# Rows of per-token numbers made by TensorE transposes of a broadcast column instead of products with the identity

## The reference, cut to what matters

```python
def _modulated_norm(h, gain, shift, scale):
    return _rms_norm(h, gain) * (1.0 + scale) + shift      # 1/root of the mean square, per token

def _l2_normalize(x):                                       # 1/length, per token and head
    xf = x.astype(jnp.float32)
    return (xf * lax.rsqrt(jnp.sum(xf * xf, axis=-1, keepdims=True) + EPS)).astype(x.dtype)

    gc = jnp.cumsum(_to_chunks(g, DN_CHUNK), axis=-1)       # cumulated log decay, per token and head
    decay = jnp.exp(jnp.where(causal, gc[..., :, None] - gc[..., None, :], -jnp.inf))
    lower = jnp.where(strict, jnp.einsum('nhcid,nhcjd->nhcij', kb, k) * decay, 0.0)
    uw = lax.linalg.triangular_solve(lower, rhs, left_side=True, lower=True, unit_diagonal=True)
    ...
    qg = q * jnp.exp(gc)[..., None]
```

## Time and profile before

| | us |
|---|---|
| median of three runs | 3181.74 |
| lowest, highest | 3181.17, 3181.83 |
| span of the profiled execution (its own time) | 3182.7 |
| PE busy | 3145.8 |
| PEld busy | 2684.8 |
| DVE busy | 1949.7 |
| ACT busy | 1276.7 |
| delta projection (about 1552 to 1757 on the trace's clock) | 205 |
| the eight steps (about 1757 to 2032) | 275 |

### The profile page before, as it was taken

How to read it: one execution, slowest core, us unless ns; L and a number is a source line. 1 busy time by engine, 2 the same in 40 slices (tenths; PEclk the granted TensorE clock), 3 DMA queues, 4 the chain that set the end, 5 groups by cost and what they waited for, 6 DMA issues and landing times.

```text
span 3182.7 us, 53025 instructions
## 1 busy us (share of the span) xinstructions
PE 3145.8 (99%) x21274; PEld 2684.8 (84%) x21274; DVE 1949.7 (61%) x2974; ACT 1276.7 (40%) x1999; POOL 97.3 (3%) x106
## 2 busy tenths in 40 slices
PE   9999999999999999999999999999999999999999
PEld 8997889889788988888788888878887888876899
DVE  6745674774467556767775777557734676347444
ACT  5444454553445452222643445442224222244433
POOL 0000000000010010000000000000000000000000
PEclk9999999999999999999999999999999999999999
DMA  7543554454345434545222000034532454211353
GB/s 270 180 151 136 190 187 165 182 185 158 133 173 188 168 128 189 194 162 197 81 80 80 3 3 3 28 142 176 210 119 79 172 193 181 99 69 40 137 182 132
DMA packets 62488, 441.25 MB, mean 139 GB/s; under 512 B 6768, under 2 KB 8944, under 8 KB 9328
## 3 DMA queue, kind: packets, MB, share of 16 engines
q1 hardware_dynamic: 60992, 437.39, 37.8%
q10 hardware_dynamic: 1328, 1.46, 0.1%
HBM read 437.77 MB, written 1.05 MB: 138 GB/s over the span
## 4 chain that ended last, share of the span: by engine, by line
PE 92%; DVE 4%; ACT 3%; issue 1%; DMA 0%; POOL 0%; DVEq 0%; ACTq 0%; SPq 0%; POOLq 0%
PE ps_high L526 47%; PE ps_low L526 44%; PE ps_high L535 1%; ACT sb_w_split L774 1%; DVE sb_w_split L811 0%; DVE sb_arena L2154 0%; PE ps_low L535 0%; DVE sb_x_split L2919 0%; ACT sb_arena L2827 0%; DVE sb_silu L2937 0%; ACT sb_xn L2818 0%; DMA sb_ring<-weights 0%; DVE sb_rinv L4506 0%; ACT L3766 0%; DVE sb_arena L2451 0%
## 5 line engine op out<-in xcount | busy, mean ns | idle before, releaser
L774 ACT ACTIVATE sb_w_split<-sb_ring 128x2048 fp32r<-128x2048 f32 x260 | 498.5, 1917 | 890.6 <-PE ps_low L526 697.5
L811 DVE TENSOR_TENSOR sb_w_split<-sb_ring,sb_w_split 128x2048 fp32r<-128x2048 f32 x260 | 597.7, 2299 | 257.0 <-ACT sb_w_split L774 257.0
L526 PE MATMUL ps_low<-sb_x_split,sb_w_split 128*128 128x512 f32 (+1 forms) x3520 | 691.4, 355 | 7.9 <-DVE sb_w_split L811 4.0
L526 PE MATMUL ps_high<-sb_x_split,sb_w_split 128*128 128x512 f32 (+1 forms) x3520 | 686.8, 354 | 0.3 <-DVE sb_w_split L811 0.3
L526 PEld LDWEIGHTS ps_low<-sb_x_split,sb_w_split 128*128 128x128 f32 x3520 | 579.5, 189 | 107.2 <-DVE sb_x_split L2919 6.1
L526 PEld LDWEIGHTS ps_high<-sb_x_split,sb_w_split 128*128 128x128 f32 x3520 | 580.8, 189 | 94.2 <-DVE sb_w_split L811 0.6
L526 PE MATMUL ps_low<-sb_a_split,sb_w_split 128*128 128x256 f32 (+1 forms) x2112 | 370.3, 325 | 0.0
L526 PE MATMUL ps_high<-sb_a_split,sb_w_split 128*128 128x256 f32 (+1 forms) x2112 | 365.8, 323 | 0.0
L526 PEld LDWEIGHTS ps_low<-sb_a_split,sb_w_split 128*128 128x128 f32 x2112 | 314.3, 190 | 37.5 <-DVE sb_w_split L811 2.8
L526 PEld LDWEIGHTS ps_high<-sb_a_split,sb_w_split 128*128 128x128 f32 x2112 | 315.0, 190 | 30.8
L1024 DVE SCALAR_TENSOR_TENSOR sb_rest<-sb_ring,sb_consts 128x1024 f32<-128x1024 f32 x256 | 313.3, 1224 | 27.1 <-DVE sb_rest L1024 7.7
(11 more groups left out here) (405 smaller groups left out, 3215.6 us busy)
## 6 DMA issues: line engine op xcount, KB each, us to landing
sb_ring<-weights SPq DMA_DIRECT2D x412, 1024.0 KB, 4.8
sb_consts<-consts SPq DMA_DIRECT2D x1, 2148.0 KB, 18.8
sb_sq<-xT SPq DMA_DIRECT2D x1, 1024.0 KB, 5.7
sb_ring<-weights SPq DMA_DIRECT2D x2, 512.0 KB, 8.0
sb_h<-ctxT ACTq DMA_DIRECT2D x1, 1024.0 KB, 14.5
out<-sb_h SPq DMA_DIRECT2D x1, 512.0 KB, 3.0
sb_vectors<-vectors ACTq DMA_DIRECT2D x1, 269.0 KB, 5.9
out<-sb_h SPq DMA_DIRECT2D x1, 256.0 KB, 2.6
```

Of the source, the lines that this page charges most:

```text
L526: ins = self.g.nc.tensor.matmul(out, lhsT, rhs, start=start, stop=stop)
L774: g.nc.scalar.activation(g.w_split[:, 0, s % 2, :], g.ring[:, n % SLOTS, :], ACT.Copy).then_inc(g.sem["w_high"], 1)
L811: g.nc.vector.tensor_tensor(g.w_split[:, 1, s % 2, :], g.ring[:, n % SLOTS, :], g.w_split[:, 0, s % 2, :].bitcast(F32), ALU.subtract).then ...
```

## The change

Every row is now made by a transpose of the broadcast column (the new helper `row`, which calls `transpose`). For the decay rows the triangular mask can't be the constant any more, so the column is taken from `gc`, where the sums are already cumulated with the opposite sign. The sign is undone behind it: the exponentials take `scale=-1.0`, and the difference subtracts and is cut off by a maximum where it added and was cut off by a minimum. PE waits once for the semaphore `decay_col`, which DVE counts up when `gc` is complete, before the first decay rows.

```diff
+    def row(self, out, column, full=None):
+        self.transpose(out, column.to_broadcast([P, P]), full)
...
 # final_rows_tensor
-            pe.mm(tile[:, t * P:(t + 1) * P], g.rinv[:, col:col + 1].to_broadcast([P, P]), g.const("identity"),
-                  full=side if t == len(cols) - 1 else None)
+            pe.row(tile[:, t * P:(t + 1) * P], g.rinv[:, col:col + 1], full=side if t == len(cols) - 1 else None)
...
 # norm_rows_tensor
-        pe.mm(tile[:, t * P:(t + 1) * P], g.rinv[:, t:t + 1].to_broadcast([P, P]), g.const("identity"),
-              full="low" if t == width // P - 1 else None)
+        pe.row(tile[:, t * P:(t + 1) * P], g.rinv[:, t:t + 1], full="low" if t == width // P - 1 else None)
...
 # length_rows
-            pe.mm(tile[:, t * P:(t + 1) * P], b["inverse_lengths"][:, at:at + 1].to_broadcast([P, P]), g.const("identity"),
-                  full="low" if t == DT - 1 else None)
+            pe.row(tile[:, t * P:(t + 1) * P], b["inverse_lengths"][:, at:at + 1], full="low" if t == DT - 1 else None)
...
+def four_rows(pe, side, column):
+    pe.wait_ge(pe.g.sem[side + "_free"], pe.tiles[side] - 3)
+    tile = pe.open(side)
+    for h in range(GH):
+        pe.row(tile[:, h * P:(h + 1) * P], column(h), full=side if h == GH - 1 else None)
...
 def decay_rows(pe, b, s, d):
     head, t = place(s)
-    four_products(pe, "high", lambda h: b["g_tok"][:, CHUNK_ORDER[d][t], d, head + h:head + h + 1].to_broadcast([P, P]),
-                  lambda h: pe.g.const("not_before")[:, d, :])
+    if s == 0 and d == 0:
+        pe.wait_ge(pe.g.sem["decay_col"], pe.due("decay_col"))
+    four_rows(pe, "high", lambda h: b["gc"][:, CHUNK_ORDER[d][t], d, head + h:head + h + 1])
...
 # out_rows
-        four_products(pe, side, lambda h: b["inverse_lengths"][:, c * GH + h:c * GH + h + 1].to_broadcast([P, P]),
-                      lambda h: g.const("identity"))
+        four_rows(pe, side, lambda h: b["inverse_lengths"][:, c * GH + h:c * GH + h + 1])
...
 # row_decays (ACT)
-    g.nc.scalar.activation(b["row_decay"][:, d, :], tile[:, :], ACT.Exp).then_inc(g.sem["row_decay"], act.adds("row_decay"))
+    g.nc.scalar.activation(b["row_decay"][:, d, :], tile[:, :], ACT.Exp, scale=-1.0).then_inc(g.sem["row_decay"], act.adds("row_decay"))
...
 # decays (ACT)
-    g.nc.scalar.activation(b["decays"][:, d, :], b["decays"][:, d, :], ACT.Exp).then_inc(g.sem["decay"], act.adds("decay"))
+    g.nc.scalar.activation(b["decays"][:, d, :], b["decays"][:, d, :], ACT.Exp, scale=-1.0).then_inc(g.sem["decay"], act.adds("decay"))
...
 # log_decays (DVE)
-    per_head(dve, lambda h, c: v.tensor_scalar(b["decays"][:, d, c], tile[:, c], head_column(b, "gc", s, d, h), 0.0, ALU.add, ALU.min),
+    per_head(dve, lambda h, c: v.tensor_scalar(b["decays"][:, d, c], tile[:, c], head_column(b, "gc", s, d, h), 0.0, ALU.subtract, ALU.max),
```

## The result

The changed kernel takes 3164.38 us (median of 4 runs, 3162.99 to 3166.10) against 3181.78 of the kernel before on the same chip (4 runs, 3181.17 to 3182.68): a ratio of 0.9941, interval 0.9930 to 0.9953, 17.4 us less. The forecast was 3163.7, 18.0 less.

What follows compares the result with a forecast made beforehand. PE, busy 99% of the span, was taken to bound the kernel. Projection 7.8, steps 7.2, last output rows 0.45 and norms 2.5 sum to 18.0 us, so 3181.7 - 18.0 = 3163.7; range 3160.0 to 3171.0.

Steps and rivals of the forecast that it cites:

- The price of a row: On PE, a product costs 0.2225 us and a transpose 0.11, so each row saves 0.112 us.
- The projection: 64 length rows and step 0's 8 decay rows save 8.1 us, less 0.25 at the end: 7.8.
- Ordinary steps: Steps 0, 1, 3, 5: decay rows at levels 3 and 4 gain 0.35 and 0.34, 0.69 each, 2.8 together.
- Closing steps: Steps 2, 4, 6, with output rows: L4160 comes 1.2 us earlier, PE goes on 1.48 earlier each, 4.4 together.
- Last output rows and norms: After step 7 only the first tile counts, 0.45 us; norm groups of four 0.45 each, the group of two 0.25.
- The seam: Six norm rows at the seam: only the low bank's four rows count, gaining 0.45 us.
- Nothing else was touched: ACT's scale and DVE's subtract and max cost nothing, L4066 stays 343 ns, PE's `decay_col` wait is already satisfied, no DMA moves.
- the rival of the clock: Transposes hold PE's clock less well; two falls a step, 16 in all, cost 26 us: 3189.8, slower; chance 0.05.
- All of it passes: Rival: all 184 rows at 0.112 and some 25 cheaper first loads count, 21.9 us, 3159.8; chance 0.07.
- The steps keep their time: Rival: DVE or ACT sets the steps, so their 7.2 us falls away: 3170.9; chance 0.10.
- Half a transpose: Rival: a row streams at 0.056 us; projection gains 11.7, norms 3.7, last rows 0.7, steps 7.2: 3158.4; chance 0.02.
- nothing at all: Rival: a transposed broadcast column costs PE 0.2225 us like the product, leaving 3181.7; chance 0.04.

Runs made afterwards that it cites:

- the length rows alone: The kernel before with only the projection's 64 length rows made by transposes: 3176.87 us, ratio 0.9981.
- the doubled rows: The changed kernel with every row transposed twice: 3182.79 us, ratio 0.9999 against the kernel before.
- the repeat: The changed kernel run again unaltered, with a second profile: 3164.99 us, ratio 0.9941 against the kernel before.
- early table load: The changed kernel with the exponential table loaded early on ACT in steps 0, 2, 4, 6: 3166.03 us; in closing steps placed behind level 3's copies instead: 3161.66 us.
- deferred multiplications: The changed kernel with DVE's two output gate multiplications in steps 2, 4, 6 moved behind the level 4 and 5 updates: 3163.77 us; with early table load too: 3159.92 us.
- the norm rows: The kernel before with only the 24 rows of the norms and the seam made by transposes: 3180.40 us, ratio 0.9988.
- the decay rows: The kernel before with only the decay rows transposed, with their sign, semaphore and ALU operations: 3178.42 us, ratio 0.9987.
- the fillers: The changed kernel with every 256-column filler product replaced by four 128-column transposes: 3164.93 us, ratio 0.9944 against the kernel before.
- the single parts: Four versions of the kernel before, each with only norm and seam, length, decay or output rows transposed: 3180.40, 3176.87, 3178.42, 3178.14 us.
- the output rows: The kernel before with only the output rows made by transposes: 3178.14 us, ratio 0.9987.

## Why the prediction was right, and where not

**The price of a row** was right: a saving of 0.112 foretold and 0.1116 measured in the length rows alone, a cost of 0.11 foretold and measured by the doubled rows. A broadcast column costs no more to transpose than the tiles of the earlier trace rows, 0.11 too. The Trainium skill, TensorE: Matmul & The Clock Gate, section Terms, gives the transpose mode a factor of four for FP32. The runs show two: two transposes took the time of one product, 7.22 us for the tile of 7.26.

**A step of its reasoning was misread.** I took the tile from 1723.42 to 1732.46 for one with 16 rows. Its second eight are key products, which the change leaves alone; they happen to cost the same, so the price came out right. But the sign I named, "with 16 after 7.3 instead of 9.04", fails as put: that tile takes 8.14. The tile that does have 16 rows takes 7.24 instead of 9.06.

**The projection**: 8.06 for 7.8. The 0.25 that I took off for L3962's idle time was not lost; 72 rows at 0.112 come through in full.

**Ordinary steps**: 0.77, 0.72 and 0.71 for 0.69 in steps 0, 1 and 3, with the turn that was foretold: PE goes on 0.15 behind L4170, which is late next. In step 5 the forecast was wrong: it took level 3 of step 3 for all four steps, but in step 5 L4160 had already set the next products, and the step gained 0.38, all of it at level 4. That the table shows 0.75 there is the luck of a pause in the profile of before.

**Closing steps**: the term that was mis-sized, 1.69 for 1.48. The mechanism holds (L4076 comes earlier until it meets DVE's own work, then L4170 sets PE), but L4076 came 1.39 earlier, not 0.97 + 0.26 = 1.23, rounded to 1.2. I had added two idle times, and each counts from the shown end of DVE's instruction before, while DVE starts the next one a little ahead of that end when nothing holds it. In step 2 after, L4170 is shown until 1824.63 and L4047 starts at 1824.56; L4049 is shown until 1827.41 and L4076 starts at 1827.33. So the first idle time of 0.26 was a slack of 0.33, and the 0.97 one of 1.05: 1.38 together, as measured. Adding idle times gives a slack that is too small by some 0.07 at each place; comparing starts gives all of it.

**Last output rows and norms**: 0.41 for 0.45, 0.51 for 0.45 and 0.28 for 0.25. The cheaper first load, which I had counted inside the steps only, would make up the 0.05; that is argued, not shown.

**The seam**: 0.1 at most for 0.45. I had read the wait of DVE for its rows and not what is late next, ACT's L2600; the profile of before, at half clock there, hides it.

**Nothing else was touched**, as foretold: L4076 at 342 ns, no idle time of PE for `decay_col` (its first decay rows follow at 1708.40 without one), the same DMA issues.

**The sum**: behind the first norm 18.28 between the two profiles and 17.9 without the pause of step 5, for 17.0; with 0.1 at the seam and some 0.45 in the first norm 18.4. Executions of equal mean clock, on the chip of the repeat, give 18.5 to 18.9: 18.9 at 0.999 (3181.49 - 3162.56), 18.7 at 0.998 (3184.91 - 3166.23), 18.5 at 1.000 (3179.28 - 3160.75), with one to seven runs in each mean. The medians of runs with different clocks give 17.4 and 17.7. So the forecast of 18.0 was 0.4 to 0.9 too small for what the change is worth. Its terms missed in both directions (closing steps 0.6 too small in all, projection and last norms 0.2 to 0.3 each, the seam 0.35 and step 5 0.3 too large), and that it lies within 0.7 us of the median is in part luck with these and with the mix of clocks. In the rival of the clock, 16 falls at a cost of 26 make 3189.7, not 3189.8. One statement of it was wrong without effect: a run's time is its span plus 1.8, so the profiled execution of before took about 3184.5 and stood 2.8 over the median, not 1.0.

**The rivals.** All of it passes: it doesn't, PE waits 0.15 behind L4170 and for ACT at the seam; the whole, at 18.4 to 18.9, lies a tenth to a quarter of the way from 18.0 to its 21.9. The steps keep their time: refuted, they gained 7.6 without the pause. Half a transpose, and nothing at all: refuted by the doubled rows. The clock: the granted clock was 1.00 over all row blocks of the projection and the steps, and also with 740 fillers transposed. The Trainium skill, TensorE: Matmul & The Clock Gate, section Part 4: PE-mode transpose, says that full clock doesn't engage for transposes; these windows don't bear that out.

Left open: what makes PE pause for 0.4 to 0.9 us in single executions, and what decides whether the clock falls at the seam.

## What to carry to other kernels

A row made from a broadcast FP32 column by a transpose costs half of the product with the identity, and where TensorE is dense all of the saving comes through; take the price from starts, not from record lengths. Read each step or level by itself before multiplying one by their number: level 3 gained 0.35 in step 3 and nothing in step 5. Where the engines meet, look for the second chain before counting on the first: here the early table load and the deferred multiplications were each worth next to nothing in a closing step and 1.1 us together. Bring a table load forward only to a place with nothing due behind it: the same call cost 0.3 us when it stood ahead of the copies.

## What the runs showed of the hardware that I had not expected

- **The granted clock falls at fixed places, at one of them not in every execution.** At about 1153 and 1525 us it stood at half for 3.4 or 6.8 us. The second fall was in all 13 profiles. The first was in those of before, the norm rows, the decay rows, the repeat and the fillers, not in the others; after and the repeat are the same program. What decides it no run here shows.
- **The times go with the clock.** Of the 31 executions of the kernel before beside the single parts, the 9 with a mean clock of 1.000 took 3179.38 us in the mean, the 8 at 0.999 3181.85, the 14 at 0.998 3185.01: 5.6 us from end to end, of a whole spread of 8.0, and a third of what the change is worth. For a change of this size, stages of profiles say more than medians of four runs, but of more than one profile on each side.
- **PE pauses in single executions.** Ahead of the rows of level 4 it paused for 0.41 us in step 5 of before, for 0.46 there with the doubled rows and for 0.42 in step 1 with the output rows, and in none of the other ten profiles. Inside a run of 64x32 products it paused for 0.66 in step 3 of the doubled rows and for 0.88 in step 0 of the fillers. The cause stays open.
- **The table load of ACT takes 1.28 us** where square root and exponential alternate. In step 0 it sat on the path: having it done earlier gave 0.87 us there. In the closing steps it was one of two chains.
